# Two more weight chunks outside the ring, half copies of the transposed x, and third-stage downs in four column tiles

## The chip, the core and the metric

One core of a Trainium2 chip (trn2) runs the kernel. Its engines are the matmul engine (PE; its weight loads are listed as PEld), the vector engine (DVE), the scalar engine (ACT), GpSimd (POOL, nearly unused here) and the sync engine (SP), which issues the weight transfers. The metric is the device time of one execution in microseconds, lower is better. All data are float32.

## The reference, cut

x is 256 tokens x 1024. Two layers of one model and one layer of another follow each other:

```
for layer in 0, 1:                      # mixers: attention variants
    x = layer_norm(alpha * x + mixer(x))
    x = layer_norm(alpha * x + moe(x))  # 4 groups x 4 experts, hidden 256
u = rmsnorm(x); h = x + mixer(u)        # gated linear + dilated attention
u = rmsnorm(h)
h = h + moe(u)                          # 4 groups x 8 experts, hidden 512
out = rmsnorm(h)

moe: g = argmax(x @ w_group); the two best experts e of group g
     y = sum_e weight_e * (silu(x @ w_gate[e]) * (x @ w_up[e])) @ w_down[e]
```

Every expert's weights are read once in each execution: 32 experts of three 2.1 MB matrices in the last layer.

## The kernel before, in words

Weights go through a **ring** of six slots of 16 KB a partition (NSLOT, `slot(n)`). One chunk (2048 KB) fills one slot. SP issues the load of chunk n when chunk n-6 is done (`chunk_done`, L592); PE waits for `slot_loaded`. The order of chunks is written out once: `expert_order(units)` gives gate 0, up 0, gate 1, up 1, down 0, gate 2, up 2, down 1, gate 3, up 3, down 2, down 3, each as two chunks, one for each of a unit's two experts. That is one **group** of the third expert stage (`moe(2)`), and there are four groups. Group 0 stands by itself in the code, groups 1 and 2 are a loop, and the last group is written again with `last=True`.

Two chunks of the last group, the downs of its unit 0, are outside the ring: `load_extra(c)` (L610) loads them ahead of the stage into storage that is free by then (EXTRA_PARTS: parts of the buffers projected, heads_transposed, mixed and norm_params). `EXTRA_AT = 8` is their place in the order. The pair of up chunks of unit 1 in group 0 is loaded in quarters (`load_in_quarters`), each as soon as the gate of unit 0 has read a quarter of its slots.

Each expert has room for 32 tokens. `hidden(kind, u)` (L1127, matmuls at L1139) computes gate or up of a unit: both experts stand side by side in two column tiles of 32 columns, the x of 32 tokens as the loaded operand, the weights as the moving one. A matmul of float32 is recorded as two instructions. `hidden_T(u)` transposes the product (L1153), DVE copies it (L2283), and `down(u, a, half)` multiplies it by the down weights: half 0 into bank 2, half 1 into bank 3, again two column tiles each (L1195). Only the very last down (L1185) puts both halves and both experts into four column tiles at once, with its half 1 in the other rows of bank 3. ACT copies bank 2 (L1715), DVE copies bank 3 (L2278). `scatter` (L1232) adds the outputs of two units to the tokens' sums in banks 4 to 7, so it does work for every second unit. Between groups `gather` (L1087) collects the tokens of the next one.

`transpose_x` (PE L728, ACT L1568, DVE L1882) transposes the 256 x 1024 x for a projection or a router: tile 0 (128 tokens) into banks 0 and 1, tile 1 into banks 2 and 3. ACT copies banks 0, 1, 2, DVE copies bank 3. PE waits for both copies of a tile before the first matmul that reads it. `keep_clock_up` issues matmuls whose result nobody reads. `project` (matmuls L769) makes the first projection of a block, `logits` (L1035) the router's.

After each expert stage a flag says whether an expert had more than 32 tokens (64 in the first two stages); then a general path runs. It does not run with these inputs.

## Time and profile before

| | us |
|---|---|
| median of three runs | 1242.79 |
| lowest, highest | 1242.15, 1244.42 |
| the profiled execution | 1239.27 |
| its span, first to last instruction | 1237.4 |
| PE busy in the span | 1155.5 (93%) |
| DVE, ACT busy | 316.2, 207.6 |
| HBM read | 362.6 MB, 294 GB/s over the span |

Times within the trace are microseconds from the span's start. Busy time is the union of the instructions of an engine; the ends of matmuls are modelled. The mean granted clock of PE is 0.99 of its full speed. The stages in order of time: first block to 305 us (its expert stage from about 175), second block to 595 (its expert stage from about 460), third block's mixer to 753, third expert stage to the end. The chain of work that ended last lies 75% on PE and 15% on DMA, 14% of it on the down weights of the third expert stage.

### The profile page before, as it was taken

How to read it: one execution, taken by the hardware profiler on the slowest of the kernel's cores; microseconds unless marked ns; L12 is line 12 of the kernel's file. 1: busy time of each engine (PE TensorE's matmuls, PEld its weight loads, DVE VectorE, ACT ScalarE, POOL GpSimd, SP SyncE). 2: the span in 40 equal slices, each digit the busy share in tenths (PEclk: the TensorE clock that was granted, in tenths of full speed). 3: DMA queues.
4: the chain of work that ended last, by engine and by line, in shares of the span. 5: the costliest groups of instructions: out<-in, count | busy, mean ns of one | idle time of the engine just before them, and what ended most of it. 6: DMA issues, size and time to landing. Idle time of an engine off the chain costs nothing.

```text
span 1237.4 us, 14481 instructions
## 1 busy us (share of the span) xinstructions
PE 1155.5 (93%) x5884; PEld 565.1 (46%) x5884; DVE 316.2 (26%) x898; ACT 207.6 (17%) x474; POOL 1.0 (0%) x6
## 2 busy tenths in 40 slices
PE   7999999999999999999899999989987998989995
PEld 3555555554687546554364545422422242233231
DVE  1466362112113343111513665100010010000002
ACT  2135321111024412111113231100000000000001
POOL 0000000000000000000000000000000000000000
PEclk9999999999999999999999999999999999999998
DMA  9794135999833133999763244799999999999994
GB/s 311 166 266 180 69 136 243 405 417 390 311 137 136 69 136 130 406 418 389 274 221 136 72 151 186 281 427 426 428 427 429 427 426 430 428 429 426 429 426 185
DMA packets 78250, 364.41 MB, mean 295 GB/s; under 512 B 21458, under 2 KB 26868, under 8 KB 53620
## 3 DMA queue, kind: packets, MB, share of 16 engines
q1 hardware_dynamic: 76724, 360.88, 74.0%
q10 hardware_dynamic: 1472, 2.78, 0.6%
q8 instruction: 38, 0.62, 0.2%
q14 instruction: 16, 0.13, 0.0%
HBM read 362.60 MB, written 1.05 MB: 294 GB/s over the span
## 4 chain that ended last, share of the span: by engine, by line
PE 75%; DMA 15%; DVE 6%; issue 2%; ACT 1%; SPq 0%; ACTq 0%; DVEq 0%
PE bank L1139 17%; DMA weights<-in_expert_w_down_dram 14%; PE bank L1195 9%; PE bank L797 8%; PE bank L819 7%; PE bank L1177 5%; PE bank L769 5%; PE bank L784 4%; PE bank L1232 3%; PE bank L1084 2%; PE bank L809 2%; PE bank L1087 2%; PE bank L847 1%; PE bank L887 1%; PE bank L1372 1%
## 5 line engine op out<-in xcount | busy, mean ns | idle before, releaser
L1139 PE MATMUL bank<-weights,projected 128*64 128x256 f32 (+1 forms) x2048 | 341.1, 489 | 17.3 <-DMA weights<-in_expert_w_up_dram 6.6
L1139 PEld LDWEIGHTS bank<-weights,projected 128*64 128x64 f32 (+1 forms) x2048 | 133.3, 124 | 209.7 <-issue 169.2
L1195 PE MATMUL bank<-weights,work 128*32 128x512 f32 x448 | 106.8, 632 | 23.4 <-DMA weights<-in_expert_w_down_dram 23.4
L797 PE MATMUL bank<-weights,x_transposed 128*128 128x512 f32 x256 | 118.6, 602 | 0.9 <-ACT heads_transposed L1629 0.9
L819 PE MATMUL bank<-weights,mixed 128*128 128x512 f32 x192 | 86.9, 599 | 1.6 <-DVE mixed L2086 1.1
L1195 PEld LDWEIGHTS bank<-weights,work 128*32 128x32 f32 x448 | 30.1, 115 | 97.7 <-issue 97.7
L769 PE MATMUL bank<-weights,x_transposed 128*128 128x512 f32 (+1 forms) x160 | 64.0, 557 | 4.8 <-ACT x_transposed L1574 3.3
L2278 DVE COPY work<-bank 64x512 f32<-64x512 f32 (+1 forms) x30 | 20.7, 689 | 184.8 <-PE bank L1195 125.3
L797 PEld LDWEIGHTS bank<-weights,x_transposed 128*128 128x128 f32 x256 | 45.7, 190 | 47.3 <-issue 45.4
L2298 DVE TENSOR_TENSOR work<-work,bank 64x512 f32<-64x512 f32 (+1 forms) x24 | 16.4, 682 | 199.0 <-PE bank L1139 199.0
L1715 ACT ACTIVATE work<-bank 128x512 f32<-128x512 f32 (+1 forms) x32 | 19.0, 594 | 250.1 <-PE bank L1195 177.7
L1232 PE MATMUL bank<-work,heads_transposed 128*128 128x512 f32 x120 | 59.9, 620 | 0.0
L1177 PE MATMUL bank<-weights,work 128*32 128x512 f32 x512 | 59.9, 597 | 0.0
L819 PEld LDWEIGHTS bank<-weights,mixed 128*128 128x128 f32 x192 | 34.9, 190 | 41.9 <-issue 39.2
L769 PEld LDWEIGHTS bank<-weights,x_transposed 128*128 128x128 f32 x160 | 29.9, 190 | 35.5 <-issue 30.1
L784 PE MATMUL bank<-x_transposed,weights 128*128 128x256 f32 (+1 forms) x208 | 45.7, 380 | 0.0
L784 PEld LDWEIGHTS bank<-x_transposed,weights 128*128 128x128 f32 (+1 forms) x208 | 38.0, 184 | 8.3 <-issue 2.0
L2283 DVE COPY work<-bank 128x256 f32<-128x256 f32 (+1 forms) x24 | 12.2, 510 | 109.1 <-PE bank L1153 109.1
L1725 ACT ACTIVATE work<-bank 64x512 f32<-64x512 f32 (+1 forms) x24 | 14.1, 589 | 150.4 <-PE bank L1139 150.4
L1232 PEld LDWEIGHTS bank<-work,heads_transposed 128*128 128x128 f32 x120 | 19.7, 188 | 40.5 <-issue 36.0
L1084 PE MATMUL bank<-heads_transposed,projected 128*128 128x128 f32 x256 | 31.9, 279 | 0.0
L1084 PEld LDWEIGHTS bank<-heads_transposed,projected 128*128 128x128 f32 x256 | 30.0, 192 | 4.0 <-issue 3.9
(315 smaller groups left out, 983.6 us busy)
## 6 DMA issues: line engine op xcount, KB each, us to landing
weights<-in_expert_w_gate_dram SPq DMA_DIRECT2D x32, 2048.0 KB, 15.7
weights<-in_expert_w_up_dram SPq DMA_DIRECT2D x30, 2048.0 KB, 16.7
weights<-in_expert_w_down_dram SPq DMA_DIRECT2D x30, 2048.0 KB, 17.3
weights<-in_moe_w_gate_dram SPq DMA_DIRECT2D x16, 2048.0 KB, 11.3
weights<-in_moe_w_up_dram SPq DMA_DIRECT2D x16, 2048.0 KB, 12.9
weights<-in_moe_w_down_dram SPq DMA_DIRECT2D x16, 2048.0 KB, 9.5
weights<-in_sb_w_in_dram SPq DMA_DIRECT2D x6, 2048.0 KB, 19.2
weights<-in_w_in_dram SPq DMA_DIRECT2D x6, 2048.0 KB, 14.9
```

Source lines behind the costliest of these rows:

```text
L769: i = mm(BANK[4 + 2 * (seq % 2) + t][:, 0:ncols], XT[:, kt, t * P:(t + 1) * P], w[:, kt, :], start=kt == 0, stop=kt == KT - 1)
L784: i = mm(BANK[4 + 2 * (seq % 2) + c // 2][0:width, (c % 2) * S:(c % 2 + 1) * S], w[:, kt, c * width:(c + 1) * width], XT[:, kt, :], start= ...
L797: i = mm(BANK[6 + t][:, :], XT[:, kt, t * P:(t + 1) * P], w[:, kt, :], start=kt == 0, stop=kt == KT - 1)
L809: i = mm(BANK[6 + half][:, c * S:(c + 1) * S], w[:, kt, (2 * half + c) * P:(2 * half + c + 1) * P], XT[:, kt, :], start=kt == 0, stop=kt = ...
L819: i = mm(BANK[bank][:, :], mixT[:, kt, t * P:(t + 1) * P], w[:, kt, :], start=kt == 0, stop=kt == KT - 1)
L1084: i = mm(to.rearrange("p (q t s) -> p q t s", t=T, s=cap)[:, :, t, :], XP[:, t, kt, :], place.rearrange("p (q s) -> p q s", s=cap), start= ...
L1087: i = mm(to, XP[:, t, kt, :], place, start=t == 0, stop=t == T - 1)
L1139: i = mm(b[n_slots * c:n_slots * (c + 1), e * F:(e + 1) * F], x[:, kt, q * n_slots:(q + 1) * n_slots], w[c][:, col:col + F], start=kt == 0 ...
L1177: i = mm(BANK[2 + half][cap * q:cap * (q + 1), :], hT[:, e * step + f, s0:s0 + cap], slot(n + c)[:, col:col + CH], start=f == 0, stop=f == ...
L1195: i = mm(BANK[2 + half][r0 + n_slots * c:r0 + n_slots * (c + 1), :], hT[:, a * step + f, n_slots * c:n_slots * (c + 1)], extra_weights(c, ...
L1232: i = mm(BANK[4 + 2 * t + half][:, :], w, YS[:, block % 2, half, :], start=False, stop=last and (SPLIT[L] or final))
L2278: cp(YS[r0:r0 + rows, (pair // 2 if rows < P else pair) % 2, 1, :], BANK[3][from0:from0 + rows, :]).then_inc(y1_ready, 1)
```

## The change

1. Two more chunks of the last group, the downs of its unit 1, are loaded ahead of the stage: into the last 2560 columns of the constants, the gate weights of the linear attention, half of a norm parameter buffer, x transposed and x itself. The constants are reordered so that those still read afterwards are in front. `EXTRA_AT` becomes (8, 14), and the last group has 20 chunks in the ring in place of 22. SP waits for the norm's second tile (`normed`) before one part and for the rank matmuls (`rank_psum`) before the last chunk.
2. `transpose_x` is split: `xt_copied` waits for the first half's copy before column block 0 and for the second half's before block 4. `project_first` makes the first projection of the second and third blocks; in the second it transposes tile 1 before the last two column blocks of tile 0, in the third before tile 1.
3. All downs of the third stage that read ring slots run in four column tiles, as the last one did. The downs of units 0 and 1 of the last group, which read the storage outside the ring, keep two.
4. In the third stage the moving operand of `keep_clock_up` is a small parameter, since the constant it read is overwritten. The general path takes its sums, its zeros and its transposed x from ring slots.

The diff, cut to its core:

```diff
-EXTRA = 2
-EXTRA_AT = 8
+EXTRA_AT = (8, 14)
 def chunk_no(L, j, last):
-    return N_MOE[L] + j - (EXTRA if L == 2 and last and j > EXTRA_AT else 0)
+    return N_MOE[L] + j - (2 * sum(j > at for at in EXTRA_AT) if L == 2 and last else 0)
...
+        SPENT = CONST_W - 5 * CH
         EXTRA_PARTS = [[PJ[:, 4096:6144], QK[:, 1536:3584]],
-                       [MIX[:, 0:2048], NORM_[:, 1024:2048], NORM_[:, 3072:4096]]]
-        def extra_weights(c, kt):
-            parts = EXTRA_PARTS[c]
-            if c == 0:
-                return parts[kt // 4][:, kt % 4 * CH:(kt % 4 + 1) * CH]
-            return parts[0][:, kt * CH:(kt + 1) * CH] if kt < 4 else parts[kt // 2 - 1][:, kt % 2 * CH:(kt % 2 + 1) * CH]
+                       [MIX[:, 0:2048], NORM_[:, 1024:2048], NORM_[:, 3072:4096]],
+                       [CONSTS[:, SPENT:CONST_W], GATE_W[:, 0:CH], NORM_[:, 2048:3072]],
+                       [XT_[:, 0:2048], X_[:, 0:2048]]]
...
+                def load_extra(c, parts):
+                    for p, part in enumerate(EXTRA_PARTS[c]):
+                        at, cols = sum(v.shape[1] for v in EXTRA_PARTS[c][:p]), part.shape[1]
+                        if p in parts:
+                            sp.dma_start(part, expert_source(L, "down", (G - 1) * 2 * units + c)[:, at:at + cols]).then_inc(extra_loaded[c // 2], 16)
                 if L == 2:
                     for j in range(4):
                         load_unit_chunk(0, j)
                     sp.wait_ge(pv_done, len(AB_JOBS) + len(DIL_JOBS))
-                    load_extra(0)
+                    load_extra(0, (0, 1))
+                    load_extra(2, (0, 1))
                     for j in range(4, 6):
                         load_unit_chunk(0, j)
-                    load_extra(1)
+                    load_extra(1, (0, 1, 2))
+                    sp.wait_ge(normed, tile_no(5, 1))
+                    load_extra(2, (2,))
+                    sp.wait_ge(rank_psum, NMOE)
+                    load_extra(3, (0, 1))
...
-                        if j // 2 != EXTRA_AT // 2:
+                        if 2 * (j // 2) not in EXTRA_AT:
...
+            def xt_copied(k, t, kt):
+                if kt == 0:
+                    pe.wait_ge(xt_act, 3 * k + 2 * t + 1)
+                elif kt == 4 and t == 0:
+                    pe.wait_ge(xt_act, 3 * k + 2)
+                elif kt == 4:
+                    pe.wait_ge(xt_dve, k + 1)
...
+            def project_first(n, seq, k, src, second_at):
+                pe.wait_ge(proj_copied, seq - 1)
+                pe.wait_ge(normed, tile_no(NORM_OF_XT[k], 0))
+                transpose_tile(src, 0)
+                chunk_loaded(n)
+                w = slot(n).rearrange("p (k c) -> p k c", k=KT)
+                for t in range(T):
+                    for kt in range(KT):
+                        if t * KT + kt == second_at:
+                            pe.wait_ge(normed, tile_no(NORM_OF_XT[k], 1))
+                            transpose_tile(src, 1)
+                        xt_copied(k, t, kt)
+                        i = mm(BANK[4 + 2 * (seq % 2) + t][:, :], XT[:, kt, t * P:(t + 1) * P], w[:, kt, :], start=kt == 0, stop=kt == KT - 1)
+                i.then_inc(chunk_done, 1)
...
-                            if extra and u == 0:
-                                pe.wait_ge(extra_loaded, 16 * sum(len(parts) for parts in EXTRA_PARTS))
+                            if extra and u < 2:
+                                pe.wait_ge(extra_loaded[u], 16 * sum(len(parts) for parts in EXTRA_PARTS[2 * u:2 * u + 2]))
                             else:
                                 load("down", u)
...
-                            pe.wait_ge((xc_act, xc_dve)[half], g * (gathers // 2) + (gather0 // 2 + gathers))
+                            for s_ in (xc_act, xc_dve) if quads else ((xc_act, xc_dve)[half],):
+                                pe.wait_ge(s_, g * (gathers // 2) + (gather0 // 2 + gathers))
...
-                        elif last and u == units - 1:
+                        elif not (extra and u < 2):
                             for f in range(step):
                                 for hh in range(2):
                                     for c in range(2):
...
-                            down(u - 1, 0, 1)
+                            if extra and u in (1, 2):
+                                down(u - 1, 0, 1)
                             scatter(u - 1, 0, 0)
                             scatter(u - 1, 0, 1)
...
-                    if last and quads:
+                    if quads:
                         down(u, 0, 0)
-                        scatter_last(u)
+                        if last:
+                            scatter_last(u)
+                        else:
+                            scatter(u, 0, 0)
+                            scatter(u, 0, 1)
                         return
...
-            transpose_x(2, by_k(X), lambda t: pe.wait_ge(normed, tile_no(NORM_OF_XT[2], t)),
-                        lambda t: project(N_SB, CH, 6, tiles=(t,)))
+            project_first(N_SB, 6, 2, by_k(X), KT - 2)
...
-            transpose_x(4, by_k(U), lambda t: pe.wait_ge(normed, tile_no(NORM_OF_XT[4], t)),
-                        lambda t: project(N_2, CH, 12, tiles=(t,)))
+            project_first(N_2, 12, 4, by_k(U), KT)
```

## Rows read from the trace of the kernel before

**Rows 1.** Part 2 of the page: GB/s moved, 40 slices of 30.9 us.
```profile
GB/s 311 166 266 180 69 136 243 405 417 390 311 137 136 69 136 130 406 418 389 274 221 136 72 151 186 281 427 426 428 427 429 427 426 430 428 429 426 429 426 185
```

**Rows 2.** Windows: length, busy PE, PEld, DVE, ACT, POOL, clock, DMA share, GB/s.
```profile
765.00:770.00 5.00, 4.43 (x19) 2.06 (x17) 4.01 (x22) 1.49 (x2) 0.00 (x0) 1.00 0.07 26
...
800.00:805.00 5.00, 5.00 (x26) 1.67 (x24) 0.42 (x1) 0.59 (x1) 0.00 (x0) 1.00 0.49 138
...
1150.00:1200.00 50.00, 47.06 (x213) 14.74 (x214) 4.01 (x7) 3.71 (x6) 0.00 (x0) 1.00 1.01 428
```

**Rows 3.** Groups of the third expert stage, 800 to 1238 us, PE.
```profile
L1139 PE MATMUL bank<-weights,projected 128*32 128x512 f32 x940 | 208.6, 597 | 13.7 <-DMA weights<-in_expert_w_up_dram 6.6 <-DMA weights<-in_expert_w_gate_dram 5.5 <-issue 1.7
L1195 PE MATMUL bank<-weights,work 128*32 128x512 f32 x448 | 106.8, 632 | 23.4 <-DMA weights<-in_expert_w_down_dram 23.4
...
L1185 PE MATMUL bank<-weights,work 128*32 128x512 f32 x32 | 3.6, 595 | 0.5 <-DVE work L2283 0.5
```

**Rows 4.** SP's DMA issues in order: start us, us, what was issued.
```profile
776.42 6.01 SPq L607 DMA_DIRECT2D weights<-in_expert_w_up_dram  x8
...
802.26 0.80 SPq L593 DMA_DIRECT2D weights<-in_expert_w_gate_dram  x2
...
1134.98 0.80 SPq L593 DMA_DIRECT2D weights<-in_expert_w_up_dram  x2
...
1196.80 0.81 SPq L593 DMA_DIRECT2D weights<-in_expert_w_down_dram  x2
```

**Rows 5.** DMA issued at 802.66, us to landing (last number).
```profile
weights<-in_expert_w_gate_dram SPq DMA_DIRECT2D x1, 2048.0 KB, 13.4
```

**Rows 6.** DMA, the pair issued at 1134.98: median us to landing.
```profile
weights<-in_expert_w_up_dram SPq DMA_DIRECT2D x2, 2048.0 KB, 11.8
```

**Rows 7.** DMA, the pair issued at 1196.80: median us to landing.
```profile
weights<-in_expert_w_down_dram SPq DMA_DIRECT2D x2, 2048.0 KB, 19.5
```

**Rows 8.** Timeline: end of the rank matmuls, gate of unit 1 in group 0.
```profile
768.43 0.39 PE L1067 MATMUL bank<-work,consts 128*128 128x32 f32 x2
...
795.20 7.06 PE L1139 MATMUL bank<-weights,projected 128*32 128x512 f32 x32 [0.70 <-issue]
```

**Rows 9.** Timeline of the last group and the tail.
```profile
1150.01 7.06 PE L1139 MATMUL bank<-weights,projected 128*32 128x512 f32 x32
...
1196.73 0.75 PE L1153 MATMUL bank<-consts,work 128*128 128x128 f32 x4
1199.53 7.06 PE L1139 MATMUL bank<-weights,projected 128*32 128x512 f32 x32 [2.05 <-DMA weights<-in_expert_w_up_dram]
1209.32 8.60 PE L1195 MATMUL bank<-weights,work 128*32 128x512 f32 x32 [2.73 <-DMA weights<-in_expert_w_down_dram]
...
1219.50 0.42 DVE L2283 COPY work<-bank 128x256 f32<-128x256 f32 x1 [0.86 <-PE bank L1153]
...
1219.97 3.64 PE L1185 MATMUL bank<-weights,work 128*32 128x512 f32 x32 [0.52 <-DVE work L2283]
```

**Rows 10.** Window of the start of the down at 1209.32.
```profile
1210.00:1212.50 2.50, 2.50 (x8) 0.63 (x6) 0.00 (x0) 0.00 (x0) 0.00 (x0) 0.51 1.00 426
```

**Rows 11.** Timeline around the first projections of the second and third blocks.
```profile
310.72 1.08 ACT L1574 ACTIVATE x_transposed<-bank 128x512 f32<-128x512 f32 x2 [2.96 <-PE bank L733]
...
311.85 7.13 PE L769 MATMUL bank<-weights,x_transposed 128*128 128x512 f32 x16 [0.73 <-ACT x_transposed L1574]
...
320.77 7.11 PE L769 MATMUL bank<-weights,x_transposed 128*128 128x512 f32 x16 [0.90 <-ACT x_transposed L1574]
...
611.51 0.60 ACT L1574 ACTIVATE x_transposed<-bank 128x512 f32<-128x512 f32 x1 [2.96 <-PE bank L733]
...
612.82 7.11 PE L769 MATMUL bank<-weights,x_transposed 128*128 128x512 f32 x16 [0.90 <-ACT x_transposed L1574]
```

**Rows 12.** Timeline before the router of the first expert stage.
```profile
175.12 1.02 PE L749 MATMUL bank<-consts 128*128 128x512 f32 x2
...
176.23 1.93 PE L1035 MATMUL bank<-small_params,x_transposed 128*128 128x20 f32 x16
```

105 lines of the change are left out of this document (59 added, 46 removed).

## Prediction

> **What bounds the kernel now.** I read the strip of 40 slices first. The first 26 slices move 69 to 418 GB/s, the last 14 hold 426 to 430 until the very end [rows 1]. So the kernel has two parts with different limits. In the third expert stage it is DMA: its share between 1150 and 1200 us is 1.01, at 428 GB/s [rows 2]. Ahead of it, as the shares of the chain show (in the text on the profile above), it is the matmul engine, PE: of the chain's 15% on DMA, 14% are the down weights of the third stage.
>
> Then the groups of the third stage: its matmuls wait for weights 23.4 us at the downs, 12.1 us at gate and up [rows 3]. A pair of chunks (one matrix of a unit's two experts) is 4.194 MB, at 428 GB/s 9.8 us. A unit is three pairs, 29.4 us. PE needs less: 7.06 us each for gate and up [rows 9], 106.8 / 14 = 7.6 us for the down [rows 3], and for scatter, transposes and its share of the gather, by my estimate from the timeline, about 4 us: 26 us.
>
> Last the tail, in order of time [rows 9]. The up of unit 3 waits for its weights until 1199.53, the down of unit 2 until 1209.32, and the last down starts at 1219.97, after its operand's copy at 1219.50. Its own two chunks, issued at 1196.80 and 0.4 later with a median of 19.5 us to landing [rows 4, 7], land 4.9 us apart: the second is there at 1197.2 + 19.5 + 2.25 = 1218.95. So both limits are near each other there. From 1219.97 to the span's end, 1237.4, lie 17.4 us of last down, scatter, norm and store, which the change leaves alone.
>
> **The stage's end: two chunks fewer through the ring.** The down chunks of unit 1 of the last group now come ahead of the stage. The stream without a gap starts with the issue at 802.26; in the 5 us from 800 the DMA share is still 0.49 [rows 2, 4]. That issue waits for the gate of unit 1 in group 0, which the change doesn't touch. Two chunks less make the stream 9.8 us shorter.
>
> Will PE follow? Its last wait for DMA becomes the up of unit 1 in the last group. That pair is issued at 1134.98 and 0.4 later with a median of 11.8 us to landing [rows 4, 6]; the second chunk is there at 1135.4 + 11.8 + 2.25 = 1149.4. PE took it at 1150.01. From there to the end of unit 3's gate at 1196.73 PE ran 46.7 us without a wait for DMA [rows 9], the down of unit 1 included. That down is still in two column tiles and now reads extra storage, as unit 0's did within the same 46.7 us. So that gate ends at 1149.5 + 46.7 = 1196.2. Then transposes 0.7, the up 7.0 (its weights are there 9.8 us sooner, so its wait of 2.05 goes), and the down of unit 2 in four column tiles at 3.6, the price of the one down that has that form now [rows 3]: 1207.5. From the end of that down (1209.32 + 8.60) to the start of the next at 1219.97 pass 2.05 us of copy, transpose and copy [rows 9]: 1209.6.
>
> The last pair's chunks give the other bound. Their issue waits for the same gate: 1196.80 before [rows 4], 1196.3 after. The pair issued at 802.26, into a nearly empty queue, had its second chunk at 802.66 + 13.4, 13.8 us after the first issue [rows 4, 5]: 1210.1. The later bound counts, so the last down starts at 1210.1 in place of 1219.97: **9.9 us**. The new limit is PE and a late slot together, 0.5 us apart.
>
> The windows show 428 GB/s. The Trainium skill, DMA: Bandwidth & Descriptors, section Where 436 GB/s comes from, says that for HBM to SBUF the HBM side, about 358 GB/s for a core, binds; by it the two chunks would be 11.7 us of stream, and the whole gain near 14.5. The trace disagrees with the page.
>
> **Downs in four column tiles.** 13 downs go from 7.0 to 3.6 us: all but the last of the stage, which has the form, and the two from extra storage. In groups 0 to 2 this gives nothing by itself, since PE waits for DMA there; the 3.4 us at the down of unit 2 are in the sum. It costs a wait: both halves end together, so a scatter waits for both copies, some 0.8 us (1217.92 to 1218.7 in the tail) [rows 9] where the other half's matmuls hid them. Cover: the 3 us of slack in each unit and the 3.4 gained. Without it, 8 scatters would cost 7 us.
>
> **What is loaded earlier.** 1.5 MB more follow the parts that are loaded now after the last attention. Ahead of them in need stand only the gate chunks of unit 1, which PE starts at 795.20 [rows 8]. 0.5 MB wait for the norm, and the last 2 MB for the rank matmuls, which end at 768.8 [rows 8]; they take 4.9 us. The DMA share between 765 and 770 is 0.07 [rows 2], and the quarters start at 776.42 [rows 4]. SP has two more waits in its queue; behind them stand the quarters, which PE frees later than both. I take nothing. Bounds: 0, and 4.9 us if the 2 MB push all behind them.
>
> **Half copies.** PE begins with the first half of the transposed x.
> - Second block's first projection: it starts after the first of two ACT copies, 1.08 - 0.60 = 0.48 us sooner, and the transposes of tile 1 move ahead of the last two column blocks of tile 0, which cover the wait of 0.90 us before the second part [rows 11]. 1.4 us, all on the PE chain.
> - Third block's: the 0.5 us of the first part are hidden by the norm of tile 1; the second part starts after the copy that ends at 612.11, not at 612.82 [rows 11]. 0.6 us.
> - Three routers: the last matmul that keeps the clock up issues from 175.12 and is through 0.86 us later (two at 0.43; 16 of the same shape take 7.1 us with the last one's tail [rows 11]), the logits start at 176.23 [rows 12]: 0.25 us each, 0.75 in all.
>
> Together **2.75 us**. Bounds: 0 if each wait reappears at a copy, 4.8 us if the 0.5 us counted everywhere.
>
> **The sum.** 9.9 + 2.75 = 12.6 us. Span 1237.4 to 1224.8; profiled execution 1239.27 to 1226.7. The median of the runs, 1242.79, is 3.5 us above that execution; taken from the median: **1230.2**. About 0.2% (2.5 us) is what a measurement of this kernel can tell from no change.
>
> **Rivals.**
> 1. *A clock fall on the new path.* The down that waited until 1209.32 took 8.60 us, not 7.06, at a granted clock of 0.51, the lower level, 1.2 GHz [rows 9, 10]. In groups 0 to 2 a fall has slack. On the path lie the wait before the up of unit 1 (9.8 - 7.06 - 0.7 = 2 us) and those before the last down. One or two falls cost 1.5 to 3 us; with half copies that give 1 us the gain is 7 to 10: 1233 to 1236. Against it: the wait of 2.05 us before 1199.53 has no fall behind it, 7.06 us [rows 9]. The Trainium skill, TensorE: Matmul & The Clock Gate, section HAM oscillation, says that where the work per tile is shorter than the wait for DMA every tile starts at the low clock; here the waits are the shorter side, and the trace has both outcomes. Chance 0.20.
> 2. *The early loads cost what they save.* The 2 MB after the rank matmuls, or a slot that comes free late, hold the stream back by 4.9 us or more. Against it: 0.07 of DMA used there. Gain 3 to 8: 1235 to 1240. Chance 0.06.
> 3. *Slower.* PE falls to 1.2 GHz in the longer waits of the last group and stays there. The chain from 1149.5 to the last down holds 60 us of work at the full clock; each us of work done at the lower one takes one more. The 12.6 are gone when 12.6 us of it are done so (25 us spent at 1.2 GHz), and half of it gives 1242.8 + 30 - 12.6 = 1260. Against it: the fall shown lasted about 3 us (1.54 lost at half), and from 1149.5 on PE has no wait. Chance 0.04.
> 4. *More.* All half copies count and the last pair is there at 1208.5: gain 15 to 17, 1226 to 1228. Chance 0.06.
>
> **How the numbers follow.** The forecast, 1228 to 1233, has 0.64. Range 1226.5 to 1236.5: the forecast, rival 1 and most of rival 4. Faster by over 0.2% (under 1240.3): all but rival 3 and an edge of rival 2, 0.93. Within 0.2%: 0.03. Slower: 0.04.
>
> **What the changed profile would show.** The downs of the ring as one form at about 3.6 us for 32 instructions; loads into constants, gate weights, x and its transpose, the last of them landed before the quarters start; a stream with no gap from 800 until the last group's unit 3; the last down at about 1207.4 by the new clock (1210.1 less 2.75), within 1 us of its chunks' landing; no gap of 0.9 us in the first projection. I am wrong if a gap of more than a us opens in the stream before that, if the up of unit 1 in the last group doesn't wait for DMA, or if the clock is at 0.5 in the last 60 us.

## The result: 1229.3 us, and the profile after

The changed kernel takes **1229.3 us** (median of four executions, 1227.99 to 1234.02) against 1243.1 (median of four, 1242.15 to 1244.42) for the one before on the same chip: ratio 0.9894, 95% interval 0.9869 to 0.9919. The forecast was 1230.2. Three later comparisons gave 0.9919, 0.9908 and 0.9916 with medians of 1229.7, 1230.2 and 1233.0. Over all four there are 22 executions, in two groups: 12 lie between 1226.8 and 1230.7 us, 10 between 1232.6 and 1237.6. What makes the upper group is the one thing that the prediction had nothing on. The first profiled execution (1234.02, span 1232.2) is of the upper group, that of the run `after_again` (1227.82, span 1226.0) of the lower one. I read the lower one first.

The strip, GB/s in 40 slices of 30.6 us, answers [rows 1]: 427 to 429 in slices 28 to 38, then 421 and 180. Slice 27 is already at 383. (Before, slices 27 to 39 held 426 to 430 and the last one moved 185, so the prediction's "last 14 until the very end" counts one slice too many.)

```profile
GB/s 313 169 252 198 69 138 208 406 413 396 359 138 119 87 112 110 407 410 403 327 206 148 76 121 292 321 383 427 427 428 428 427 428 429 429 429 428 427 421 180
```

PE's groups in the third expert stage, 760 us to the end (columns as in [rows 3]). Line numbers have moved: gate and up are L1173, the downs from the ring L1220, those from extra storage L1230, the scatter L1267.

```profile
L1173 PE MATMUL bank<-weights,projected 128*32 128x512 f32 x1024 | 233.0, 608 | 36.6 <-DMA weights<-in_expert_w_gate_dram 20.2 <-DMA weights<-in_expert_w_up_dram 14.2 <-issue 1.5
L1220 PE MATMUL bank<-weights,work 128*32 128x512 f32 x448 | 63.8, 704 | 24.6 <-DMA weights<-in_expert_w_down_dram 21.9 <-DVE projected L2306 2.6
L1267 PE MATMUL bank<-work,heads_transposed 128*128 128x512 f32 x56 | 25.9, 605 | 4.2 <-ACT work L1757 4.2
```

The downs from the ring went from 106.8 to 63.8 us of PE, 43 us less, and in groups 0 to 2 nothing of it was gained: PE's waits for gate and up weights grew from 12.1 to 34.4. The scatters now wait 4.2 us for copies, six times 0.7, inside the same slack. Each down of 32 instructions takes 3.6 us at the full clock, or 5.0 to 5.3 where the clock was at its lower level for part of it.

The issues of SP that open the stream and end it (as [rows 4]), then the stage's first gate and the end of the stage (as [rows 8, 9]):

```profile
800.26 0.80 SPq L596 DMA_DIRECT2D weights<-in_expert_w_gate_dram  x2
...
1192.81 0.80 SPq L596 DMA_DIRECT2D weights<-in_expert_w_down_dram  x2
```

```profile
772.47 1.05 PE L1173 MATMUL bank<-weights,projected 128*32 128x512 f32 x4 [0.69 <-ACT projected L1785]
...
1147.50 7.06 PE L1173 MATMUL bank<-weights,projected 128*32 128x512 f32 x32 [2.04 <-DMA weights<-in_expert_w_up_dram]
...
1204.80 0.72 PE L1187 MATMUL bank<-consts,work 128*128 128x128 f32 x4 [0.90 <-ACT work L1757]
1206.94 5.34 PE L1220 MATMUL bank<-weights,work 128*32 128x512 f32 x32 [1.42 <-DMA weights<-in_expert_w_down_dram]
1213.19 3.67 PE L1250 MATMUL bank<-work,heads_transposed 128*128 128x512 f32 x8 [0.91 <-DVE work L2326]
```

Three stretches are enough to compare executions: to the first gate of the stage (before: 774.47), from there to the start of the last down (445.5), and from that to the end of the span (17.4). The table gives all executions that were profiled; each kernel in it is explained below.

| profiled execution | first gate | gate to last down | last down to end | gate to end |
|---|---|---|---|---|
| before | 774.5 | 445.5 | 17.4 | 462.9 |
| after, four executions | 778.9, 772.5, 773.8, 780.9 | 434.3, 434.5, 434.7, 435.0 | 19.1, 19.1, 17.4, 17.4 | 453.4, 453.6, 452.0, 452.4 |
| half_only | 771.8 | 446.6 | 17.4 | 464.0 |
| two_tiles | 781.0 | 436.9 | 17.4 | 454.3 |
| one_pair, one_old | 772.0, 772.0 | 444.2, 444.2 | 19.0, 20.0 | 463.1, 464.3 |
| fill_end, late_fill | 774.0, 772.0 | 436.0, 436.0 | 17.4, 17.4 | 453.4, 453.4 |
| late_only, late_old | 773.5, 771.5 | 434.6, 434.8 | 17.4, 17.4 | 452.0, 452.2 |
| general_old | 771.4 | 434.7 | 18.8 | 453.5 |

So the change is worth 10.5 to 11.2 us from the first gate to the last down, in the four profiled executions of it, against the one profiled execution of before. half_only, whose third stage is that of before, took 1.1 us more there (experiment 2 has what its trace shows), so the gain is known to about 1 us only. In two of the four the clock takes 1.7 back at the end, and what comes before the first gate spreads over 9.5 us.

### The profile page after: what moved, and what is told of

Same layout as the page of the kernel before. It is cut to its first block, busy times and chain, and to the rows that moved or that the text cites. A ratio compares the mean times of both kernels' runs of the same rounds, so it can differ in the third digit from the quotient of the medians.

```text
span 1232.2 us, 14481 instructions
## 1 busy us (share of the span) xinstructions
PE 1119.7 (91%) x5884; PEld 559.8 (45%) x5884; DVE 316.2 (26%) x898; ACT 207.5 (17%) x474; POOL 1.0 (0%) x6
## 4 chain that ended last, share of the span: by engine, by line
PE 69%; DMA 21%; DVE 6%; issue 2%; ACT 1%; SPq 0%; ACTq 0%; DVEq 0%
DMA weights<-in_expert_w_down_dram 16%; PE bank L1173 16%; PE bank L825 8%; PE bank L847 7%; PE bank L1212 5%; PE bank L1220 4%; PE bank L812 4%; DMA weights<-in_expert_w_up_dram 4%; PE bank L1267 3%; PE bank L800 3%; PE bank L1118 2%; PE bank L837 2%; PE bank L789 2%; PE bank L1121 1%; PE bank L875 1%
## 5 line engine op out<-in xcount | busy, mean ns | idle before, releaser
L1173 PE MATMUL bank<-weights,projected 128*64 128x256 f32 (+1 forms) x2048 | 346.4, 494 | 42.3 <-DMA weights<-in_expert_w_gate_dram 23.5
L1173 PEld LDWEIGHTS bank<-weights,projected 128*64 128x64 f32 (+1 forms) x2048 | 136.6, 124 | 237.2 <-issue 191.6
L1220 PE MATMUL bank<-weights,work 128*32 128x512 f32 x448 | 60.7, 674 | 24.4 <-DMA weights<-in_expert_w_down_dram 21.8
L825 PEld LDWEIGHTS bank<-weights,x_transposed 128*128 128x128 f32 x256 | 45.9, 191 | 46.4 <-issue 45.6
L1267 PE MATMUL bank<-work,heads_transposed 128*128 128x512 f32 x120 | 59.9, 620 | 4.2 <-ACT work L1757 4.2
L1212 PE MATMUL bank<-weights,work 128*32 128x512 f32 x512 | 59.9, 597 | 0.0
L1220 PEld LDWEIGHTS bank<-weights,work 128*32 128x32 f32 x448 | 17.7, 121 | 63.4 <-issue 62.1
L1267 PEld LDWEIGHTS bank<-work,heads_transposed 128*128 128x128 f32 x120 | 19.7, 188 | 45.1 <-issue 34.3
L1767 ACT ACTIVATE work<-bank 64x512 f32<-64x512 f32 (+1 forms) x24 | 14.1, 589 | 153.9 <-PE bank L1173 153.9
L800 PE MATMUL bank<-weights,x_transposed 128*128 128x512 f32 (+1 forms) x96 | 37.4, 551 | 1.5 <-DMA weights<-in_ab_w_in_dram 1.5
## 6 DMA issues: line engine op xcount, KB each, us to landing
weights<-in_moe_w_gate_dram SPq DMA_DIRECT2D x16, 2048.0 KB, 11.1
```

The lines of the kernel that those rows point to most:

```text
L800: i = mm(BANK[4 + 2 * (seq % 2) + t][:, 0:ncols], XT[:, kt, t * P:(t + 1) * P], w[:, kt, :], start=kt == 0, stop=kt == KT - 1)
L825: i = mm(BANK[6 + t][:, :], XT[:, kt, t * P:(t + 1) * P], w[:, kt, :], start=kt == 0, stop=kt == KT - 1)
L1173: i = mm(b[n_slots * c:n_slots * (c + 1), e * F:(e + 1) * F], x[:, kt, q * n_slots:(q + 1) * n_slots], w[c][:, col:col + F], start=kt == 0 ...
L1212: i = mm(BANK[2 + half][cap * q:cap * (q + 1), :], hT[:, e * step + f, s0:s0 + cap], slot(n + c)[:, col:col + CH], start=f == 0, stop=f == ...
L1220: i = mm(BANK[2 + hh][r0:r0 + n_slots, :], hT[:, f, n_slots * c:n_slots * (c + 1)], slot(n + c)[:, col:col + CH], start=f == 0, stop=f == ...
L1267: i = mm(BANK[4 + 2 * t + half][:, :], w, YS[:, block % 2, half, :], start=False, stop=last and (SPLIT[L] or final))
```

## Experiments

**1. The changed kernel again** (no edit).

> The changed kernel once more, for a profile of another execution. Theory A (the prediction's working): the 3.8 us stall within the first transposes of the second block and the 2.2 us that the profiled execution was late before it belong to that execution alone; here the second block's first projection has no gap over 1 us and the span is about 1226 us. Rival B: the stall belongs to the new code (a wait or instructions that arrive late), it comes again, and the half copies of the second block then give nothing. For the third stage both expect 434 to 436 us from its first gate to its last down (445.5 before), and the last down again at the lower clock, 5.3 us in place of 3.6.

Measured: 1229.66 us (1227.68 to 1237.60, six executions), ratio 0.9919 (0.9893 to 0.9945). The profiled one has no stall; these are PE's rows of the second block's start in it, and below them the same place in the first profiled execution of the same code:

```profile
310.81 1.20 PE L738 MATMUL bank<-consts,residual 128*128 128x128 f32 x8 [0.77 <-DVE residual L1967]
312.34 5.39 PE L789 MATMUL bank<-weights,x_transposed 128*128 128x512 f32 x12 [0.33 <-ACT x_transposed L1616]
317.57 1.05 PE L738 MATMUL bank<-consts,residual 128*128 128x128 f32 x8
...
327.04 1.24 PE L812 MATMUL bank<-x_transposed,weights 128*128 128x256 f32 x5
```

```profile
312.26 0.35 PE L738 MATMUL bank<-consts,residual 128*128 128x128 f32 x1 [0.64 <-DVE residual L1967]
316.44 1.65 PE L738 MATMUL bank<-consts,residual 128*128 128x128 f32 x7 [3.83 <-issue]
318.02 6.10 PE L789 MATMUL bank<-weights,x_transposed 128*128 128x512 f32 x12
```

There PE does one of eight transposes, stands for 3.83 us without waiting for anything that the profile shows (`<-issue`), and then works at the lower clock for a while (six column blocks, 12 instructions of 0.43 us, take 6.10 instead of 5.39). In the lower group the block runs from 310.81 to 327.04, 16.2 us, against 17.75 before; with the stall it takes 21.2. So the stall isn't in every execution: theory A for this one, though its "that execution alone" falls with the later runs. But it had to be asked why 10 of 22 are in the upper group.

**2. Half copies alone**, on the kernel before:

```diff
+                        xt_copied(k, t, kt)
                         i = mm(BANK[0][:, t * 64:t * 64 + NR], XT[:, kt, t * P:(t + 1) * P], router_w[L][:, kt, :],
...
-            transpose_x(2, by_k(X), lambda t: pe.wait_ge(normed, tile_no(NORM_OF_XT[2], t)),
-                        lambda t: project(N_SB, CH, 6, tiles=(t,)))
+            project_first(N_SB, 6, 2, by_k(X), KT - 2)
...
+            project_first(N_2, 12, 4, by_k(U), KT)
```

> The kernel before with the half copies alone: project_first in the second and third blocks and the two waits in the routers. Theory A: 2.75 us faster than before, ratio 0.9978 (1.4 us at the second block, 0.6 at the third, 0.25 at each of three routers). Rival B: the first projection of the second block gives nothing or costs, and the whole gives 1.35 us or less, ratio 0.999 or above.

Measured: 1237.63 us against 1241.04 (eight and twenty executions), ratio 0.9964 (0.9952 to 0.9977), which is 2.9 to 6.0 us; 2.75 lies just below. The trace gives the parts:

```profile
174.63 1.16 PE L731 MATMUL bank<-consts,residual 128*128 128x128 f32 x8 [0.41 <-DVE residual L1943]
175.62 1.02 PE L757 MATMUL bank<-consts 128*128 128x512 f32 x2
176.48 1.75 PE L1061 MATMUL bank<-small_params,x_transposed 128*128 128x20 f32 x15
...
310.23 1.13 PE L731 MATMUL bank<-consts,residual 128*128 128x128 f32 x8 [0.77 <-DVE residual L1943]
311.70 5.39 PE L782 MATMUL bank<-weights,x_transposed 128*128 128x512 f32 x12 [0.33 <-ACT x_transposed L1598]
316.92 1.05 PE L731 MATMUL bank<-consts,residual 128*128 128x128 f32 x8
...
326.39 1.89 PE L805 MATMUL bank<-x_transposed,weights 128*128 128x256 f32 x8
...
609.09 1.16 PE L731 MATMUL bank<-consts,mixed 128*128 128x128 f32 x8 [1.10 <-DVE mixed L1951]
610.49 1.98 PE L782 MATMUL bank<-weights,x_transposed 128*128 128x512 f32 x4 [0.24 <-ACT x_transposed L1598]
```

Second block: 16.16 us from 310.23 to 326.39 in place of 17.75, 1.59 gained, and the gap of 0.90 is gone. Third block's second part: 1.40 after the transposes' start, before 2.06, 0.66 gained. Router: its logits follow the last clock-keeping matmul after 0.86 us in place of 1.11 [rows 12], 0.25, and the same 0.25 in the later two. Together 3.0, theory A's parts. The first gate stands at 771.8 in place of 774.5.

One thing of this trace bears on the third stage, which is that of before. A down of group 1 runs long for the clock, and some 15 us later the stream has a gap: 370 GB/s in 5 us, where before has 423 (window as in [rows 2]).

```profile
980.18 9.99 PE L1221 MATMUL bank<-weights,work 128*32 128x512 f32 x32 [3.33 <-DMA weights<-in_expert_w_down_dram]
```

```profile
1005.00:1010.00 5.00, 5.00 (x16) 1.70 (x14) 0.69 (x1) 0.00 (x0) 0.00 (x0) 1.00 0.97 370
```

It took 2.9 us more than 7.06, about the slack of a unit (some 3 us by the prediction's estimate), and the last down of the stage comes 1.1 us later than in before (446.6 and 445.5). I read the gap as the cause; no run isolates it. The prediction's "in groups 0 to 2 a fall has slack" holds, by this reading, for the shorter falls only.

**3. Downs in two column tiles**, early chunks and half copies kept (the first line has the main edit; waits, calls and the rows that DVE copies from follow it):

```diff
-                        elif not (extra and u < 2):
+                        elif last and u == units - 1:
```

> The changed kernel with the downs of the third stage in two column tiles again (the very last one has four, as before). Theory A: in groups 0 to 2 nothing is lost, since PE waits for weights there; in the last group the down of unit 2 is 3.4 us longer on the path and its scatter's wait of 0.8 us goes, so it is 2.5 to 3.4 us slower than the changed kernel and some 9.5 us faster than before. Rival B: the shorter downs make PE's waits longer, and with them more falls of its clock, which costs what they save: the time is within 1 us of the changed kernel's. In the trace of the changed kernel nine steps ran at the lower clock, before it six; by B it is six or fewer here.

Measured: 1236.19 us (1229.58 to 1237.53, six executions), ratio 0.9938 (0.9914 to 0.9961). The median says 6.5 us slower than the changed kernel, but its profiled execution has a stall of 3.52 us at the second block and one of 2.25 at the third; its first gate stands at 781.0. From the gate on:

```profile
1208.76 7.04 PE L1230 MATMUL bank<-weights,work 128*32 128x512 f32 x32
1216.63 0.72 PE L1187 MATMUL bank<-consts,work 128*128 128x128 f32 x4 [0.83 <-issue]
1217.86 2.35 PE L1220 MATMUL bank<-weights,work 128*32 128x512 f32 x20 [0.52 <-DVE work L2326]
```

The down of unit 2 takes 7.04 us, no weights are waited for behind it, and the last down comes 2.3 us later than in the changed kernel (436.9 and, on average of the four, 434.6 after the gate): PE is the limit. That is just under theory A's 2.5 to 3.4. What B said of the clock is true too. Four downs of the stage ran long for the clock here (B had six or fewer), eleven steps in `after_again`, and the mean granted clock shows it (windows as in [rows 2], first two_tiles, then after_again):

```profile
800.00:1200.00 400.00, 363.31 (x1599) 121.95 (x1599) 33.58 (x55) 21.81 (x38) 0.00 (x0) 0.98 1.00 424
```

```profile
800.00:1200.00 400.00, 334.62 (x1606) 114.68 (x1606) 32.15 (x53) 23.46 (x39) 0.00 (x0) 0.95 1.00 425
```

A PE that is done sooner waits longer, and its clock falls more often. Most of these falls lie in slack. The one at the very last down does not: where it happens, four column tiles are worth 0.8 us from gate to end (454.3 against 453.4 and 453.6), where it doesn't, 2 (452.0 and 452.4).

**4. One pair outside the ring**, half copies and four column tiles kept:

```diff
-EXTRA_AT = (8, 14)
+EXTRA_AT = (8,)
...
-                    load_extra(2, (0, 1))
...
-                    sp.wait_ge(normed, tile_no(5, 1))
-                    load_extra(2, (2,))
-                    sp.wait_ge(rank_psum, NMOE)
-                    load_extra(3, (0, 1))
```

> The changed kernel with only the one pair of chunks outside the ring that the kernel before has; half copies and four column tiles stay. Theory A: the stream of weights sets the stage's end, and the last pair lands some 9.8 us later than in the changed kernel; the four column tiles alone give 0 to 1 us there, the half copies 2.75. So it is 9 us slower than the changed kernel and 3 to 3.8 us faster than before. Rival B: the four column tiles alone give 3 us at the end of the stage, so it is 6 us slower than the changed kernel.

Measured: 1242.49 us, ratio 1.0008 (0.9985 to 1.0031), so the same as before in spite of the half copies. Again two groups, and wider apart: six executions from 1236.1 to 1240.6, six from 1244.4 to 1247.5. The profiled one, 1237.04, is of the lower group:

```profile
1206.40 4.98 PE L1215 MATMUL bank<-weights,work 128*32 128x512 f32 x32 [3.16 <-DMA weights<-in_expert_w_down_dram]
...
1216.19 2.79 PE L1215 MATMUL bank<-weights,work 128*32 128x512 f32 x12 [3.21 <-DMA weights<-in_expert_w_down_dram]
```

Both last downs wait over 3 us for weights and run at the lower clock. From gate to last down it is 444.2 (and again 444.2 in one_old), and 434.3 to 435.0 with the second pair outside: **9.6 us for one pair of chunks**, theory A for the stage. Its total, 3 to 3.8 us faster than before, holds for the lower group only. Four column tiles without the second pair give 1.3 us at the last down against before, 2.4 against half_only, and lose 1.6 to the clock behind it: from gate to end 463.1, between the 462.9 of before and the 464.0 of half_only. And what the two loads cost ahead of the stage shows here as well: the issue that opens the stream follows the first gate after 27.79 us in `before`, in this kernel and in the changed one alike.

**5. The changed kernel a third time**, beside the next three.

> The changed kernel a third time, beside the three variants of it, for the spread of its executions. So far four of its six latest lay at 1227.7 to 1230.7 us and two at 1234.6 and 1237.6. Theory A: the lower ones are what the code takes, the upper ones have a stall like the 3.8 us at the second block's transposes; median 1228 to 1230, about two of ten above 1233.

Measured: 1230.18 us (1226.76 to 1234.59), ratio 0.9908 (0.9887 to 0.9930); three of six are in the upper group. In its profiled execution the last down started after the same two waits as in after_again, the second one even longer, and there was no fall; PE's rows of after_third, and below them the granted clock during the last down of after_again (windows as in [rows 2]):

```profile
1205.87 0.72 PE L1187 MATMUL bank<-consts,work 128*128 128x128 f32 x4 [0.90 <-ACT work L1757]
1208.46 3.64 PE L1220 MATMUL bank<-weights,work 128*32 128x512 f32 x32 [1.87 <-DMA weights<-in_expert_w_down_dram]
```

```profile
1208.00:1209.00 1.00, 1.00 (x12) 0.39 (x8) 0.00 (x0) 0.00 (x0) 0.00 (x0) 0.50 0.00 0
```

So the fall at the end is a matter of the execution, not of the code; two of four profiled executions have it.

**6. PE kept busy at the end:**

```diff
+                            if extra and u == units - 1:
+                                pe.wait_ge(h_ready, g * units + (unit0 + u + 1))
+                                keep_clock_up(2, 1, moving)
                             scatter(u - 1, 0, 0)
...
                         hidden_T(u)
                         if L < 2:
                             keep_clock_up(1, 3)
+                        else:
+                            keep_clock_up(3, 1, moving)
```

> The changed kernel with matmuls whose result nobody reads in PE's two waits before the very last down: two before the transposes (in the wait of 0.90 us for a copy) and three after them (in the wait of 1.42 us for the weights). Theory A: the last down took 5.34 us because the granted clock fell to its lower level after those waits; kept busy, PE takes 3.6 us for it, and the kernel is 1.7 us faster than the changed one. Rival B: the fall comes from the waits that lie farther back or comes one step later, in the scatter; then it is the same, or up to 0.5 us slower because the last filler delays the down.

Measured: 1230.70 us (1229.07 to 1234.41), ratio 0.9915 (0.9898 to 0.9933), not to be told from the changed kernel.

```profile
1205.05 1.98 PE L764 MATMUL bank<-small_params,consts 128*128 128x512 f32 x4
1206.87 0.63 PE L1187 MATMUL bank<-consts,work 128*128 128x128 f32 x4
1207.34 2.74 PE L764 MATMUL bank<-small_params,consts 128*128 128x512 f32 x6
1210.01 3.64 PE L1220 MATMUL bank<-weights,work 128*32 128x512 f32 x32
```

The clock stays up, the down takes 3.64, but it starts at 436.0 after the gate in place of 434.5. I had counted 0.43 us for each filler; two take 1.82 us until the transposes can start, three 2.67 until the down can, since each is two instructions of 0.43. The fillers became the limit and gave 1.5 us of the 1.7 back. So theory A is right on the clock and wrong on the time, and rival B the other way round.

**7. The last pair without a slot to wait for.** Its chunks go into the storage that the last group's first down has read, with the fillers (late_fill) and without (late_only):

```diff
+                        if j >= per_group - 2:
+                            if j == per_group - 2:
+                                sp.wait_ge(extra_psum, 1)
+                            for p, part in enumerate(EXTRA_PARTS[j % 2]):
+                                at, cols = sum(v.shape[1] for v in EXTRA_PARTS[j % 2][:p]), part.shape[1]
+                                sp.dma_start(part, expert_source(L, "down", (G - 1) * 2 * units + 2 * (units - 1) + j % 2)[:, at:at + cols]).then_inc(last_loaded, 16)
-                        if 2 * (j // 2) not in EXTRA_AT:
+                        elif 2 * (j // 2) not in EXTRA_AT:
                             load_unit_chunk(G - 1, j, True)
```

> fill_end, and the last pair of chunks goes into the storage that the last group's first down has read by then, so its issue waits for that down and no longer for the gate of unit 3. Theory A: the slot was late by little, the DMA share was 0.98 before that issue, and the stream itself is the limit: the pair lands 0.5 to 1 us sooner, and the kernel is 0.5 to 1 us faster than fill_end. Rival B (the prediction put the late slot and the 13.8 us from issue to landing on the path as a limit of their own): the issue some 15 us sooner lets the pair land 3 us sooner, PE's chain becomes the limit, and it is 1 us faster from the landing and more from the clock.

> The changed kernel with the last pair in the storage that the last group's first down has read, so that it is issued some 15 us sooner, and with no matmuls added. Theory A: what fill_end and late_fill lost was the added matmuls themselves, 1.56 us of delay against 1.7 us of clock; the pair is there 1.5 us sooner, PE's chain of copy, transposes and copy becomes the limit, 0.9 us ahead of the changed kernel's last down, and with a wait of only 0.5 us before the down the clock stays up: 1 us faster by the shorter wait, 2.6 us with the clock where the changed kernel falls. Last down at 433.5 us after the stage's first gate and 3.6 us long. Rival B: the clock falls all the same after the wait of 0.90 and 0.5 us; then 0.9 us faster at most.

Measured: late_fill 1227.71 us (1227.23 to 1229.89, four executions), ratio 0.9888 (0.9873 to 0.9903); late_only 1231.23 (1227.62 to 1234.61), ratio 0.9915 (0.9896 to 0.9935), and the changed kernel beside it 1232.96. In the trace late_fill is at 436.0, limited by its fillers like fill_end, so it can't tell its two theories apart. late_only (its line numbers are seven to nine higher):

```profile
1179.03 0.43 SPq L646 DMA_DIRECT2D projected<-in_expert_w_down_dram  x1
...
1180.46 0.91 SPq L646 DMA_DIRECT2D norm_params<-in_expert_w_down_dram  x2
```

```profile
1205.97 0.72 PE L1194 MATMUL bank<-consts,work 128*128 128x128 f32 x4 [0.90 <-ACT work L1767]
1208.14 0.59 PE L1229 MATMUL bank<-projected,work 128*32 128x512 f32 x1 [1.45 <-DMA norm_params<-in_expert_w_down_dram]
```

The pair is issued at 1179.0, 405.5 us after the first gate where the changed kernel issues it at 420.3, and its last part is there at the same time: the down starts at 434.6. An issue 15 us sooner moved nothing, since other transfers were ahead of it all the time (DMA share 1.01 from 1150 to 1195 us): the stream itself is the limit. The theories on late_only, one with the pair there 1.5 us sooner, one with 0.9 us gained, both fall, and so does the prediction's reading of a late slot. The medians of these two kernels differ by the spread, not by what stands here: late_only has three of six executions above 1232 us, late_fill none of four.

**8. The code that is jumped over.** The change lengthens the general path of all three expert stages (transposes, copies and a clearing of zeros), though only the third needs it. PE jumps over this path just ahead of the places with stalls. general_old gives the first two stages their old path back:

```diff
-                    for t in range(T):
-                        for kt in range(KT):
-                            i = nc.tensor.transpose(BANK[2 * t + kt // 4][:, (kt % 4) * P:(kt % 4 + 1) * P], XP[:, t, kt, :], ident)
-                    i.then_inc(v["xt_again"], 1)
+                    if L == 2:
+                        for t in range(T):
+                            for kt in range(KT):
+                                i = nc.tensor.transpose(BANK[2 * t + kt // 4][:, (kt % 4) * P:(kt % 4 + 1) * P], XP[:, t, kt, :], ident)
+                        i.then_inc(v["xt_again"], 1)
```

> The changed kernel with the general path of the first two expert stages as it was in the kernel before (it does not run with these inputs; PE jumps over it just ahead of the second block's first transposes, where the stall of 3.8 us stood). Theory A: the length of what is jumped over has no part in the stall; the same spread as the changed kernel, with about a third of the executions over 1233 us. Rival B: the longer code that is jumped over makes the stall; all executions lie within 1227 to 1231 us.

> The changed kernel beside the two variants below, on the same chip. Theory A: 1228 to 1230.5 us; of the executions some lie above 1232 us, as 6 of 16 so far.

> late_only with the general path of the first two expert stages as in the kernel before. Theory A: as late_only, with the same spread. Rival B: the code that is jumped over has a part in the stalls; then late_only has executions 4 us and more above its lowest and this one has none, as general_old had none in four.

> one_pair with the general path of the first two expert stages as in the kernel before. one_pair had 6 of 12 executions at 1244.4 to 1247.5 us and the others at 1236.1 to 1240.6. Theory A (the code that PE jumps over ahead of the second and third block has a part in the stalls, as the ten executions of general_old and late_old within 1225.8 to 1229.9 suggest): none above 1241 us, median about 1237. Rival B: the upper group of one_pair comes from its third stage, where eleven steps ran at the lower clock; then it is here too, some of the executions at 1244 us and above.

Measured, all executions in us:

| | with the long path in all stages | with the old path in the first two |
|---|---|---|
| changed kernel | 22 executions, 1226.8 to 1237.6, ten above 1232 | 4, 1226.7 to 1229.5 (ratio 0.9892, 0.9877 to 0.9906) |
| last pair early | 6, 1227.6 to 1234.6, three above 1232 (0.9915) | 6, 1225.8 to 1229.9 (ratio 0.9885, 0.9867 to 0.9904) |
| one pair | 12, 1236.1 to 1247.5, six above 1244 (1.0008) | 11, 1236.5 to 1240.4 (ratio 0.9978, 0.9966 to 0.9991) |

Beside the run late_old the changed kernel took 1232.96 (1228.75 to 1236.10), ratio 0.9916 (0.9894 to 0.9939), above the 1228 to 1230.5 expected. None of the 21 executions with the old path is in an upper group, against 19 of 40 with the long one. (The kernels with the long path that have no partner: two_tiles four of six above 1232 us, fill_end three of six, late_fill none of four. half_only, with the old path, has none in eight, 1235.8 to 1239.5.) That the code has a part in it is shown, by three pairs of kernels that differ in nothing else; two of the pairs ran side by side, one_old later than one_pair on the same chip. What it does is only half seen. Six stalls stand in the profiled executions, all in kernels with the long path: 3.83, 3.83 and 3.52 us at the second block (after, after_fourth, two_tiles), 2.22, 2.25 and 2.25 at the third (after_fourth, two_tiles, one_pair). In all six a packet of 16 KB comes in on q8, one of two queues that load instructions, in a stretch where the weights hold the DMA engines full. It starts between 0.3 us before PE stops and 1.3 us after, and PE goes on 1.40 to 1.48 us after its end: in after PE stands from 312.61 to 316.44 and the packet takes from 313.87 to 314.96. Queues between 313 and 314 us: with the stall, and below it the same window of after_again.

```profile
q1 hardware_dynamic: 187, 0.38, 103.9%
q8 instruction: 1, 0.02, 6.8%
```

```profile
q1 hardware_dynamic: 185, 0.38, 102.9%
```

At the third block after_fourth stands among its clock-keeping matmuls:

```profile
605.84 3.68 PE L764 MATMUL bank<-consts 128*128 128x512 f32 x4 [2.22 <-issue]
```

All three executions with the stall at the second block are of an upper group and have that packet between 313 and 314. one_pair, with a stall at the third block alone, is of its lower group (1237.04). Of the eleven others, nine have the packet earlier, between 302 and 308. Not all fit so neatly: one_old and late_old have it at 311.9 and 311.3 and no stall. I take it that PE stands because its next instructions are not there, and that the code decides where it runs out of them; the packets speak for the first and the spread for the second. The runs don't show why only half of the executions are hit, nor whether it is the length of the path or the places where the packets cut the code.

A further 1.7 to 2.4 us by which executions differ is there within the first 30 us. PE's first projection up to 30 us, in after_again and in after_third:

```profile
11.97 18.26 PE L800 MATMUL bank<-weights,x_transposed 128*128 128x512 f32 x42 [1.82 <-DMA weights<-in_ab_w_in_dram]
```

```profile
11.88 18.31 PE L800 MATMUL bank<-weights,x_transposed 128*128 128x512 f32 x38 [1.47 <-DMA weights<-in_ab_w_in_dram]
```

Six profiled executions get through 37 or 38 instructions there (after, after_third, after_fourth, two_tiles, fill_end, late_only), the eight others through 42 or 43. In the six the trace's first record of the full clock starts at 15.4 to 16.3 us, in the eight at 9.7 to 11.1. So PE comes to its full clock some 5 us later in them; why is open.

By ratio the fastest kernels are late_old (1227.9 us, 0.9885), late_fill (1227.7, 0.9888) and general_old (1228.6, 0.9892), which the spread doesn't tell apart; all keep the two chunks, the half copies and the four column tiles.

## Why the prediction was right

**The bound.** Right, and more strictly than I put it: in the changed kernel the last down waits for the stream, and the slot behind its load is no limit of its own. A pair measured 9.6 us. The Trainium skill, DMA: Bandwidth & Descriptors, section Where 436 GB/s comes from, says that for HBM to SBUF about 358 GB/s for a core binds. By it a pair would be 11.7 us, an estimate, and no run here comes near that.

**The stage's end, 9.9 us.** Measured 10.5 to 11.2 (434.3 to 435.0 against 445.5), 10.9 on average. One pair is worth 9.6 by experiment 4, as the 9.8 us of a pair at 428 GB/s had it. The point "up of unit 1 in the last group" was right to 0.1 us: 375.0 us after the first gate, as forecast. The 46.7 us from there to the end of unit 3's gate were 45.2, the term that was mis-sized. The rows show where: the down of unit 1, out of extra storage, starts while the up of unit 2 still runs.

```profile
1169.92 5.77 PE L1173 MATMUL bank<-weights,projected 128*32 128x512 f32 x26
1175.11 0.62 PE L1230 MATMUL bank<-consts,work 128*32 128x512 f32 x1
1175.11 0.62 PE L1230 MATMUL bank<-x_transposed,work 128*32 128x512 f32 x1
1175.52 0.60 PE L1173 MATMUL bank<-weights,projected 128*32 128x512 f32 x2
```

It begins 5.19 us after that up; from the ring, in the trace of before, it began 6.56 us after it:

```profile
1172.43 7.06 PE L1139 MATMUL bank<-weights,projected 128*32 128x512 f32 x32
1178.99 7.06 PE L1195 MATMUL bank<-weights,work 128*32 128x512 f32 x32
```

Up and down stand in different column tiles in both, and in the first the matmuls alternate. The down of unit 0, also out of extra storage but in the column tiles of the up before it, begins 6.86 us after that up (1154.36 and 1147.50 in after_again). So by these rows the other column tiles have a part in it. That the wait for the slot is what keeps the ring's down back is argued from this one pair of rows, not shown. The Trainium skill, TensorEngine Tiling (Array Packing), section Key Properties, says that different tiles can load and multiply in parallel; by these rows they do, for 1.4 us.

**"PE and a late slot together, 0.5 us apart".** This reading was wrong, though its number wasn't. The bound of 13.8 us from issue to landing came out right (14.1) because the transfers ahead of the pair took about that long; experiment 7 shows that the slot isn't what it waits for. Had I worked from the stream alone, 9.8 us off the landing at 1218.95, I would have had 1209.15, 434.7 after the gate: the measured value. The gain exceeds 9.8 because before PE's chain ended 1 us behind the landing, and now it ends ahead of it.

**Four column tiles.** 3.6 us each, and nothing in groups 0 to 2 by themselves, as said; what they add there is slack, which half_only seems to have lacked once. At the end I had 3.4; two_tiles gives 2.3 at the last down. New is that they raise the number of clock falls, which takes most of it back in two of the four profiled executions.

**Early loads at nothing.** Right: 27.79 us from first gate to the opening issue, before and after.

**Half copies, 2.75.** 3.0 by the rows, 2.9 to 6.0 by the ratio.

**Rival 1**, the clock on the new path, came true at its price in two of the four profiled executions: 5.34 for 3.64 at the last down, at a granted clock of 0.50. I had set it against the forecast as one or the other; it is both, by the execution, and its time of 1233 to 1236 is reached, where it was profiled (after, after_fourth), with the stall and not by the fall alone. The prediction also named a clock of 0.5 in the last 60 us as a sign of being wrong. That sign stands in these two executions, though a fall of 1.7 us is small beside a gain of 13.8. The wait of 2 us before the up of unit 1 was there as described in after_again and left the clock alone; in after_third it was 0.56, behind a gate that a fall had stretched to 8.54. **Rivals 2, 3 and 4** didn't occur.

**What was missing.** The sum from the profiled execution, 1226.7, was the lower edge of the lower group (1226.8 to 1230.7); the shift of 3.5 us to the median stood for a spread of before whose cause no run shows. The changed kernel's median fell near the forecast because 10 of its 22 executions are in an upper group. The two of them that were profiled have a stall at the second block and reach the first gate 5 and 7 us later than after_third, which was as late as they were at 30 us. The change itself brought this in, in a part that I had left out as not running with these inputs. The predicted median is right to 1 us partly by luck: about 1 us more gained in the stage and 0.25 more in the half copies, 0.85 back on average from the clock (1.7 in two of four), and the stall on top.

## What to carry to other kernels

Where a stream of weights runs without a gap, count bytes: a pair of chunks taken out is worth its share of the stream, and neither slots nor issue times matter until the queue runs dry. Work taken off an engine that waits for that stream buys slack and longer waits, and these can cost clock just where the stream ends. Code that never runs is still part of the program: put a path that is needed in one place only there, and compare the spread of the executions, not the median alone.

## What the runs showed of the hardware

- PE stood for 2.2 to 3.8 us, six times in fourteen profiled executions, for nothing that the profile shows, just behind a jump over a long path and with the DMA engines full. In each a packet of an instruction queue came in, and PE went on 1.40 to 1.48 us after its end. The clock was at the lower level afterwards in five of the six, not in one_pair.
- After waits of 0.90 and 1.4 to 1.9 us before the last down the granted clock fell to 0.50 in some executions (after_again, 1.42) and not in others of the same code (after_third, 1.87). By these runs a fall depends on the execution as well as on the place.
- Matmuls of an up and of the next down, in other column tiles, ran beside each other for 1.4 us (after_again, from 1175.11); in the same column tiles they did not (1154.36).
- With downs of 7.06 us in two column tiles, one that took 9.99 us for the clock was followed by a gap in the stream, 370 GB/s in place of 423 over 5 us (half_only, 1005 to 1010).
